# Two attention forms inside one Trainium2 kernel: the values become the stationary operand, and the division by the sum moves ahead of the product

## The reference

```python
def block_attention(q, k, v, blk, n_back, with_prev, sink=None):
    s = jnp.einsum('bnqhgd,bnkhd->bnhgqk', qb, kb) * (dh ** -0.5)   # masked by distance
    m = s.max(-1)                                  # mixers 0 and 3: also over the sink
    p = jnp.exp(s - m[..., None])
    l = p.sum(-1)                                  # mixers 0 and 3: + exp(sink - m)
    o = jnp.einsum('bnhgqk,bnkhd->bnqhd', p, vb) / l
    ...
def mixer_a(x, w_qkv, b_qkv, sinks, w_o, b_o, cos, sin):   # mixers 0 and 3
    ...
    return o.reshape(B, S, nq).astype(x.dtype) @ w_o + b_o
```

## Time and profile before

| | us |
|---|---|
| median of 3 runs (lowest, highest) | 2353.24 (2352.29, 2353.77) |
| profiled execution, its own time | 2353.32 |
| its span, first to last instruction | 2351.5 |
| TensorE busy | 2308.6 (98%) |
| VectorE busy | 1451.2 (62%) |
| ScalarE busy | 1306.0 (56%) |
| GpSimd busy | 328.9 (14%) |
| mean granted TensorE clock | 0.998 of full |

### The profile page before, as it was taken

How to read it: one execution, slowest core, us unless ns; L and a number is a source line. 1 busy time by engine, 2 the same in 40 slices (tenths; PEclk the granted TensorE clock), 3 DMA queues, 4 the chain that set the end, 5 groups by cost and what they waited for, 6 DMA issues and landing times.

```text
span 2351.5 us, 36560 instructions
## 1 busy us (share of the span) xinstructions
PE 2308.6 (98%) x15272; PEld 2066.8 (88%) x15272; DVE 1451.2 (62%) x2217; ACT 1306.0 (56%) x1958; POOL 328.9 (14%) x307
## 2 busy tenths in 40 slices
PE   7999999999999999999999999999999999999999
PEld 6799978888899888998789989899899898998998
DVE  6655555546645546555765467575687686765875
ACT  5554465555644556445564467565665675655654
POOL 0100032211100313001010002343000013530000
PEclk9999999999999999999999999999999999999999
DMA  6255543333455534555345554344455453444553
GB/s 266 90 208 187 180 178 135 140 139 126 179 184 193 197 135 161 194 183 197 120 165 194 186 181 153 138 164 165 179 183 194 175 184 122 166 163 161 201 193 126
DMA packets 58180, 398.92 MB, mean 170 GB/s; under 512 B 6816, under 2 KB 7072, under 8 KB 11680
## 3 DMA queue, kind: packets, MB, share of 16 engines
q1 hardware_dynamic: 56864, 393.75, 46.2%
q10 hardware_dynamic: 1152, 2.83, 0.3%
HBM read 395.51 MB, written 1.05 MB: 169 GB/s over the span
## 4 chain that ended last, share of the span: by engine, by line
PE 83%; DVE 8%; ACT 6%; POOL 2%; issue 1%; DMA 1%; SPq 0%; ACTq 0%; DVEq 0%; POOLq 0%
PE b L1280 12%; PE b L1282 12%; PE b L1281 12%; PE b L1178 12%; PE b L1179 12%; PE b L1180 12%; PE b L1183 5%; PE b L1187 4%; DVE wlo L1931 3%; ACT whi L1581 2%; PE b L1246 1%; ACT b L1577 1%; DVE xb L2230 1%; PE b L1247 1%; ACT S L1578 1%
## 5 line engine op out<-in xcount | busy, mean ns | idle before, releaser
L1931 DVE TENSOR_TENSOR wlo<-raw,whi 128x2048 fp32r<-128x2048 f32 x362 | 843.1, 2333 | 447.9 <-ACT whi L1581 447.6
L1581 ACT ACTIVATE whi<-raw 128x2048 fp32r<-128x2048 f32 x362 | 690.5, 1913 | 427.2 <-PE b L1282 231.0
L1280 PE MATMUL b<-xh,whi 128*128 128x256 f32 x2560 | 723.9, 283 | 0.6
L1282 PE MATMUL b<-xh,wlo 128*128 128x256 f32 x2560 | 712.5, 278 | 0.0
L1281 PE MATMUL b<-xl,whi 128*128 128x256 f32 x2560 | 711.5, 278 | 0.0
L1280 PEld LDWEIGHTS b<-xh,whi 128*128 128x128 f32 x2560 | 480.3, 188 | 5.2 <-DVE wlo L1931 2.7
L1281 PEld LDWEIGHTS b<-xl,whi 128*128 128x128 f32 x2560 | 481.4, 188 | 1.9
L1282 PEld LDWEIGHTS b<-xh,wlo 128*128 128x128 f32 x2560 | 481.1, 188 | 0.0
L1178 PE MATMUL b<-whi,xh 128*128 128x512 f32 x640 | 263.0, 411 | 1.5 <-DVE wlo L1931 1.5
L1178 PE MATMUL b<-whi,oh 128*128 128x512 f32 x656 | 259.1, 395 | 0.6 <-DVE ol L2221 0.6
L1179 PE MATMUL b<-wlo,oh 128*128 128x512 f32 x656 | 256.1, 390 | 0.0
(11 more groups left out here) (238 smaller groups left out, 2900.0 us busy)
## 6 DMA issues: line engine op xcount, KB each, us to landing
raw<-in_w SPq DMA_DIRECT2D x362, 1024.0 KB, 4.8
gt<-in_rows SPq DMA_DIRECT2D x8, 512.0 KB, 4.1
bt<-in_rows SPq DMA_DIRECT2D x8, 512.0 KB, 5.2
abq<-in_rows ACTq DMA_DIRECT2D x2, 768.0 KB, 6.2
x<-in_x SPq DMA_DIRECT2D x1, 1024.0 KB, 6.8
bc<-in_rows SPq DMA_DIRECT2D x4, 256.0 KB, 5.1
out<-x SPq DMA_DIRECT2D x4, 256.0 KB, 2.1
msk<-in_masks SPq DMA_DIRECT2D x1, 768.0 KB, 21.4
```

Of the source, the lines that this page charges most:

```text
L1280: pe.matmul(out, wh[:, k, cs], ah[:, kk, :], start=kk == 0 and s == 0, stop=False, skip_group_check=True)
L1282: last = pe.matmul(out, wl[:, k, cs], ah[:, kk, :], start=False, stop=final and k == 3, skip_group_check=True)
L1581: return ac.activation(out, i, ACT.Copy)
L1931: ve.tensor_tensor(B.wlo[r][:, :], B.raw[r][:, :], B.whi[s][:, :], ALU.subtract).then_inc(sem["loV"], 1)
```

## The change

It concerns mixers 0, 2 and 3 (`KIND` "a" and "c"); mixer 1 and the later layers keep their order (`LAG` 1).

- Order of a visit on TensorE: `probs(v-2)`, `pv(v-3)`, `score(v)`. A run of n pairs has n + 3 visits, before n + 2.
- `share`, new: after `score(v)`, VectorE takes the reciprocal for pair v-1 and divides the first head's exponentials in `S` in place, two instructions (128 and 256 columns); GpSimd does the same for the second head. The turn of a pair waits for both.
- `pv`: the stationary operand is 64 columns of values, the moving one 128 columns of turned exponentials. Head 0 goes to partitions 0 to 63 of the result, head 1 to 64 to 127; query half 0 stands in one bank, half 1 in the other. The result is already turned.
- `opair`, in place of `heads` and `opart`: VectorE copies both banks to `og`, ScalarE copies 256 columns to `oh`, GpSimd takes the rest `ol`. It stands last in its visit.
- The turned exponentials of odd pairs go to `og[2]`. The output projection waits for GpSimd's count `olo`.

```diff
+LAG = {"a": 2, "b": 1, "c": 2, "d": 1}
@@ Order.attention
-        for v in range(n + 2):
+        for v in range(n + lag + 1):
...
+            if turned and lag == 2:
+                self.step("probs", a, v - 2)
+            if v > lag:
+                self.step("pv", a, v - lag - 1, dv, n)
             if v < n:
                 ...
                 self.step("score", a, v, mask, kidx, ...)
...
             if v < n:
                 self.step("exp", a, v, sinks is not None)
...
+            if lag == 2 and 1 <= v <= n:
+                ...
+                self.step("share", a, v - 1)
+            if v > lag:
+                consume(v - lag - 1)
@@ mixer_a (mixer_bc alike, for mixer 2)
             def consume(v):
-                self.step("heads", u0, v, v // 4)
-            def tail(g):
-                self.out_part((i, g), g // 2)
-                ready[g] = True
+                self.out_pair(i, v, u0, v)
+                if v % 2:
+                    ready[v // 2] = True
@@ TensorE, rows_ready
+            if a // 2 in (0, 2, 3):
+                p.wait_ge("olo", mark["olo", (a // 2, 2 * blk + 1)])
@@ TensorE, probs
+            elif KIND[a] in "ac":
+                name = ("shared_v", "shared_g")[i]
+                p.wait_ge(name, mark[name, (a, v_)])
@@ TensorE, pv
+        if KIND[a] in "ac":
+            ...
+            for t, k, at in ((0, 0, 0), (1, 0, 128), (1, 1, 256)):
+                b = use["S", a, v_ + 3, t][0]
+                for i in range(2):
+                    c = 64 * (v_ // 2) if KIND[a] == "a" else 128 * p_ + 64 * i
+                    last = mm(B.bank[b][64 * i:64 * i + 64, 384:512], v[:, k, c:c + 64], B.turned(a, v_, i)[:, at:at + 128],
+                              k == 0, k == t)
@@ ScalarE
+    def opair(i, pair, first, v):
+        ...
+        copy(B.oh[:, pair, :], B.opair(pair)).then_inc(sem["ohi"], 1)
@@ VectorE
-    def heads(a, pair, hh):
+    def share(a, pair):
+        u, p = o.pair(a, pair)
+        s = p % 2
+        v.wait_ge("exp", mark["exp", (a, pair, 1)])
+        if pair >= 2:
+            v.wait_ge("shared_g", mark["shared_g", (a, pair - 2)])
+        ve.reciprocal(B.rl[:, s, 0:4], B.l[u % 4][:, 4 * p:4 * p + 4]).then_inc(sem["sums"], 1)
+        v.wait_ge("sums", mark["sums", (a, pair)])
+        S = B.S[2 * (pair % 2)]
+        for t, cs in enumerate((slice(0, 128), slice(129, 385))):
+            last = ve.tensor_scalar(S[:, cs], S[:, cs], B.rl[:, s, t:t + 1], None, ALU.mult)
+        last.then_inc(sem["shared_v"], 1)
+    def opair(i, pair, a, v_):
+        for t in range(2):
+            b, n = use["S", a, v_ + 3, t]
+            v.wait_ge(f"full{b}", n + 1)
+            ve.tensor_copy(B.opair(pair)[:, 128 * t:128 * t + 128],
+                           B.bank[b][:, 384:512]).then_inc(sem[f"empty{b}"], 1)
@@ GpSimd
+    def share(a, pair):
+        s, S = pair % 2, B.S[2 * (pair % 2) + 1]
+        g.wait_ge("sums", mark["sums", (a, pair)])
+        for t, cs in enumerate((slice(0, 128), slice(129, 385))):
+            last = ge.tensor_scalar(S[:, cs], S[:, cs], B.rl[:, s, 2 + t:3 + t], None, ALU.mult)
+        last.then_inc(sem["shared_g"], 1)
+    def opair(i, pair, a, v):
+        g.wait_ge("ohi", mark["ohi", (i, "pair", pair)])
+        ge.tensor_tensor(B.ol[:, pair, :], B.opair(pair), B.oh[:, pair, :], ALU.subtract).then_inc(sem["olo"], 1)
```

More of the change, by code:

```diff
@@ L550, in attention @@
                     self.counts("exp", (a, v, i))
[L551 to L556, removed]
+            if turned and lag == 1:
                 self.step("probs", a, v - 1)
@@ L573, in attention, with out_pair @@
             tail(g)
+    def out_pair(self, i, pair, a, v):
+        self.counts("ohi", (i, "pair", pair))
+        self.counts("olo", (i, pair))
+        self.step("opair", i, pair, a, v)
     def out_part(self, key, source):
@@ L682, in consume @@
                         if i == 2:
-                            self.step("heads", u, gr, hh)
+                            self.out_pair(i, 4 * hh + gr, u, gr)
+                            if gr % 2:
+                                ready[2 * hh + gr // 2] = True
                         else:
@@ L1401, in pv @@
             return
+        if KIND[a] in "ac":
+            for t in range(2):
+                b, n = use["S", a, v_ + 3, t]
+                p.wait_ge(*o.copied[a, v_, t])
+                p.wait_ge(f"empty{b}", n)
+            for t, k, at in ((0, 0, 0), (1, 0, 128), (1, 1, 256)):
[4 more added lines that the diff above has]
+                              k == 0, k == t)
+                if k == t and v_ + 3 >= pairs:
+                    last.then_inc(sem[f"full{b}"], 1)
+            return
         for i in range(2):
@@ L1405, in pv @@
             p.wait_ge(f"empty{b}", n)
[L1406 removed]
+            c = 128 * p_ + 64 * i
             pt, out = B.PT[i], B.bank[b][:, 384:512]
@@ L1707, in probs @@
     def probs(first, v):
-        b, n = use["T", first, v + 1, 0]
+        b, n = use["T", first, v + LAG[KIND[first]], 0]
         a.wait_ge(f"full{b}", n + 1)
-        copy(B.PT[0][:, 0:384], B.bank[b][:, 0:384]).then_inc(sem[o.copied[first, v, 0][0]], 1)
+        copy(B.turned(first, v, 0)[:, 0:384], B.bank[b][:, 0:384]).then_inc(sem[o.copied[first, v, 0][0]], 1)
     def rise(u, p):
@@ L1715, in rise @@
         act(e, e, ACT.Exp).then_inc(sem["stat_a"], 1)
+    def opair(i, pair, first, v):
+        for t in range(2):
+            b, n = use["S", first, v + 3, t]
+            a.wait_ge(f"empty{b}", n + 1)
+        copy(B.oh[:, pair, :], B.opair(pair)).then_inc(sem["ohi"], 1)
     def opart(key, source):
@@ L2147, in heads @@
         v.wait_ge("exp", mark["exp", (a, pair, 1)])
-        i = v.mine(ve.reciprocal(B.rl[:, s, 0:4], B.l[u % 4][:, 4 * p:4 * p + 4]))
-        values(a, pair, 1)
-        v.wait_ge("own_v", i)
-        for i in range(2):
-            c = 128 * p + 64 * i
-            src, gone = values(a, pair, i)
-            r = B.rl[:, s, 2 * i:2 * i + 2].unsqueeze(2).broadcast_to([128, 2, 64])
-            ve.tensor_tensor(B.og[hh][:, :, c:c + 64], src, r, ALU.mult).then_inc(sem[gone], 1)
+        if pair >= 2:
[7 more added lines that the diff above has]
+    def opair(i, pair, a, v_):
+        for t in range(2):
+            b, n = use["S", a, v_ + 3, t]
+            v.wait_ge(f"full{b}", n + 1)
+            ve.tensor_copy(B.opair(pair)[:, 128 * t:128 * t + 128],
+                           B.bank[b][:, 384:512]).then_inc(sem[f"empty{b}"], 1)
     def merge(u, p, g):
@@ L2476, in vector_program @@
             "center": center, "affine": affine, "meansq": meansq, "rms": rms, "sinks": sinks, "scale_x": scale_x, "kv_in": kv_in, "rope_v": rope_v, "q_bias": q_bias,
-            "score": score, "probs": probs, "heads": heads, "merge": merge, "rise": rise, "weights": weights,
+            "score": score, "probs": probs, "share": share, "opair": opair, "merge": merge, "rise": rise, "weights": weights,
             "opart": opart, "gate": gate, "hlo": hlo, "taps": taps, "gate2": gate2, "gm_squares": gm_squares,
@@ L2821, in sm, with turned, opair @@
         return self.small[:, a:a + n]
+    def turned(self, a, pair, i):
+        return self.og[2][:, i, :] if KIND[a] in "ac" and pair % 2 else self.PT[i]
+    def opair(self, pair):
+        return self.og[pair // 4][:, pair % 4 // 2, 256 * (pair % 2):256 * (pair % 2) + 256]
     def act(self, x):
```

45 lines of the change are left out of this document (22 added, 23 removed).

## The result

The changed kernel takes **2374.04 us** (median of 4 runs, 2373.04 to 2377.39) against 2352.76 for the kernel before (4 runs beside it): a ratio of 1.0094, 95% interval 1.0083 to 1.0106. It is 0.9% slower. The forecast was 2354 with a range of 2341 to 2366; the time lies outside it, 20 us above the number. The profiled execution took 2374.39 us, its span is 2372.6.

A forecast was written before the change was run, and what follows sets the result against it. TensorE, busy 98% of the span, was taken to bound the kernel. -9.7 - 5.2 - 4.8 + 8.2 + 3.0 + 8.0 + 1.5 = +1.0 on 2353.3 gave 2354 us; 8-in-10 range 2341 to 2366.

The forecast's parts named there:

- Relief: TensorE's visits in mixers 0, 2 and 3 shorten from 2.87 to 2.47 us (-9.7); twelve `opart` go (-5.2).
- that rival: In `pv` the column halves run one after another, 0.67 us more each, 16 in all: 2370 us; chance 0.09.
- old waits: TensorE's existing waits in mixers 0, 2 and 3, where `opart` or a turn waited for VectorE or ScalarE, go: -4.8 us.
- first turns: In mixers 0 and 3 the turns of visits 2 and 3 come late, 1.5 us each: +3.0 together.
- turns of visits 6, 7, 8: In mixers 0 and 3, behind six products, the second head's turn waits 1.2 us for GpSimd's division in each visit.
- (b): In mixers 0 and 3 the output projection's first row waits 4.0 us for the last result `ol`: +8.0 together.
- I take s + 3.0 for GpSimd: GpSimd's two divisions end 3.0 us after s, when TensorE finishes a visit's scores; ends s + 2.6 and s + 5.2.
- GpSimd is locked out: Rival: VectorE's `wlo` comes between GpSimd's two divisions and holds the second by 2.2 us: 2363 us; chance 0.14.
- a sign that the prediction is wrong: Turns waiting where 12 products lie between visits; with 12 or 18 products nothing was to be lost.
- (c): In mixer 2 one `wlo` right after `share` and one before GpSimd's last difference cost +1.5 us together, ends 0 and 4.
- (a): Turns wait for divisions behind six products: three visits each in mixers 0 and 3, one in mixer 2 (1.0): +8.2 us.
- The waits don't come or are short: Rival: GpSimd finishes at s + 2.6, shrinking the waits (about 2347), or relief counts alone (2334); put at 2343 us, chance 0.29.

The follow-up runs named there:

- Kernel 7: Only mixer 2 changed, with divisions and older sums (`opair`) issued ahead of the scores, against the kernel before: 2347.28 us, ratio 0.9978.
- Experiment 3: The changed kernel with all four divisions of a pair of visits on VectorE at the same place, none on GpSimd: 2361.63 us.
- experiment 1: The changed kernel with the divisions issued ahead of fill and score, right behind the products with the values: 2358.32 us.
- Experiments 4 and 5: The kernel before, TensorE held before the first output projection row in mixers 0 and 3 by four or two GpSimd products: 2364.86 and 2358.38 us.
- experiment 2: The changed kernel with the divisions and the older sums (`opair`) both issued ahead of the scores: 2355.93 us.
- (9): Changed kernel, divisions and older sums ahead of scores; in mixers 0 and 3 visit 4's older work no longer waits for the queries' second half: 2373.37 us.
- kernel 6: The change made in mixer 2 only, mixers 0 and 3 as in the kernel before: 2353.37 us, ratio 1.0004.

## Why the prediction was wrong

Mechanism and places of most waits were right; the sum missed 20 us because waits on divisions were priced too low, mostly through GpSimd, and because nothing stood in it for the clock. By place, measured less predicted, it missed 6.8 us in mixer 0 (9.0 against 2.2), 8.6 in mixer 3 (10.8 against 2.2), 3.6 in mixer 2 (0.1 against -3.5) and 1.3 in mixer 1, where it had no term.

**Relief: right.** The products with the values take 0.806 us, start to next start; I took 0.86. The two heads' column halves run side by side (their records start 0.01 us apart in pairs), so that rival is out. The turn takes 0.75 instead of 0.63, I had 0.65. By TensorE's blocks, mixer 0 saves 8 x (2.87 - 2.42) + 4 x 0.44 = 5.4 us; my sum has 5.0 a mixer. Kernel 7 shows it in time: mixer 2 is 5.4 us shorter there.

Mixer 0, term by term, from the distances between TensorE's starts in the changed kernel:

| | predicted | measured |
|---|---|---|
| products, transposes of `og` | -5.0 | -5.4 |
| old waits | -1.9 | -1.8 |
| first turns (visit 2: 0.8 + 2.7) | +1.5 | +3.5 |
| turn of visit 4, small ones | 0 | +1.1 |
| first row | +4.0 | +4.2 |
| turns of visits 6, 7, 8 (1.65, 1.63, 1.47) | +3.6 | +4.8 |
| half clock, twice | 0 | +3.0 |
| sum | +2.2 | +9.4 (+9.0 by the cut) |

**The first row's wait (b): right in place, and nearly in size.** 4.2 us in mixer 0 against 4.0, and the same idle time, 4.09, in mixer 3. The chain is the one forecast, VectorE's copy behind scores and divisions, ScalarE's copy behind the exponentials, then GpSimd's difference at 75.05. But GpSimd's own two divisions ended only then (73.44 + 1.64), just behind ScalarE's copy, while the forecast had them done a quarter of a microsecond ahead of it. Here are VectorE, then ScalarE, then GpSimd, of the changed kernel before the row at 75.88:

```profile
73.37 0.66 DVE L2188 TENSOR_SCALAR S<-S,rl 128x128 f32<-128x128 f32 x2
73.96 0.47 DVE L2195 COPY og<-b 128x128 f32<-128x128 f32 x2
```
```profile
74.53 0.42 ACT L1609 ACTIVATE oh<-og 128x256 fp32r<-128x256 f32 x1
```
```profile
73.44 1.64 POOL L2582 TENSOR_SCALAR S<-S,rl 128x128 f32<-128x128 f32 x2 [6.08 <-DVE rl L2184]
75.05 0.72 POOL L2587 TENSOR_TENSOR ol<-og,oh 128x256 fp32r<-128x256 f32 x1
```

**The step that failed first: "I take s + 3.0 for GpSimd".** I priced its two divisions at 1.1 to 1.3 us from a product of 256 columns and a 512-column division of 1.49. They take 1.65, so the undisturbed pair is done at s + 3.4 (64.89 + 1.65, with s at 63.17), and 3.6 where a `wlo` comes between. That is what my rival "GpSimd is locked out" said: I gave it 0.14. A `wlo` came between in four visits: in one of mixer 0 at 51.40, in one of mixer 3 (where the second head's turn came 2.7 us late as well, at 1152.95), and in mixer 2 at 849.41 and 895.53. Each pair took about 1.95 us over the undisturbed one; three of them, 5.8 us together, stood in TensorE's way, and behind the one at 849.41 TensorE stood idle for only 0.42. I had counted the late first turns as "1.5 us each" without putting that rival's price there. Experiment 3 takes GpSimd out and gains 12.4 us, experiment 1 gives the divisions a head start and gains 15.7. The list of places was short too. In mixer 2's second run visit 2 stands behind six products as visit 4 does, and turns waited behind 12 products at 899.18 and behind 18 at 853.06, which I had named as a sign that the prediction is wrong. The Trainium skill, GPSIMD Engine Reference (Specifications), says that GpSimd shares its SBUF interfaces with VectorE instructions that have two SBUF inputs. `wlo` is one, and the pair of 3.60 us around it agrees: the price here is the length of the `wlo` less the overlap.

**The step that was missing: the clock.** My waits cost their length and no more. Experiments 4 and 5 show that this is wrong by 1.6 us for a wait of 4 us, and by 1.3 to 1.5 for one of 2 us in one of two places. In the changed kernel it makes 1.5 + 1.5 us in mixer 0 (nine products over 3.7 us that take 2.2 at full clock, and the scores and products from 55.55). Mixer 3 had 13.7 us at the lower level where mixer 0 had 6.8, about 1.3 us more of it in work that TensorE had to do (products and scores ahead of the row, from 1168.03 to 1171.09, took 3.06 us in place of 1.74 in mixer 0); this is the larger part of what it lost beyond mixer 0 (10.8 against 9.0). The Trainium skill, TensorE: Matmul & The Clock Gate (Why this matters for your kernels), warns of idle gaps between bursts of products because they bring the lower clock. The trace agrees behind mixer 0's wait of 4.1 us and behind both waits of experiment 4 (in mixer 3 of the changed kernel the drop began ahead of the wait), and the page would have been grounds for a term for the two row waits that I forecast at 4.0. That waits of 2.4 us drew the drop too is in this trace.

**Mixer 2 (c):** predicted -3.5 (its share of the relief, old waits, +1.0 of (a), +1.5), measured +0.1 from the 124th to the 135th conversion. Its waits on divisions are 5.6 us by the trace, not 2.5: the first heads wait 0.6 in two visits, the second heads 0.7, 0.8, 2.0 and 0.8. That explains 3.1 of the 3.6 us. The other 0.6 is relief and old waits that I put at 6.0 and kernel 7 shows as 5.4. The remaining 1.3 us of the part up to the 135th conversion are the wait on GpSimd's rotation in mixer 1.

**One rival's number.** "The waits don't come or are short" gives 2350 by its own terms (2354.3 less seven times 0.4 and twice 0.7), not 2347. The forecast doesn't use it.

**What stays open.** Whether the sink mixers can gain at all. With the best order (2) they still lose 1.8 and 2.4 us in the profiled execution, which was 2.3 us faster than the median: row wait, visit 7 with its fill under a `wlo`, one half clock each. The row's wait could not be moved forward (9). Writing the sinks elsewhere than on GpSimd wasn't tried.

## What to carry to other kernels

When work moves ahead of the product that needs it, price the new wait at the *slowest* case of the engine it moves to, and look for what of its neighbour may come between two of its instructions; two small divisions took 0.66 us on VectorE and 1.65 to 3.6 on GpSimd. Put new producers first in their engine's visit, not behind work of a younger visit: the same instructions in that order were worth 15.7 us here. A wait of TensorE of some microseconds isn't always paid with its length alone; count a half-clock stretch behind it, 1.3 to 1.6 us each here, and take such a change stage by stage, since one stage (mixer 2, 0.22% faster) may win what the others lose.

## What the runs showed of the hardware

- Products of 64 stationary columns for two heads, on separate columns of the array: 12 f32 records in 0.806 us with 128 moving columns, against 1.38 us with the exponentials as stationary operand.
- GpSimd's fill of 4 columns took 0.19 us alone and 2.31 beside a `wlo` that had started 0.02 us earlier (experiment 2), more than the 1.25 of the earlier trace rows.
- VectorE's 256-column division took 0.46 us in the changed kernel, with GpSimd's division running beside it, and 0.35 in experiment 3, where GpSimd had none.
- The clock's drop is not fixed by one wait's length: 2.1 us of waiting was followed by it in one of two like places of the same run, and 1.77 us on a turn in mixer 2 in kernel 6 but not in the changed kernel. In experiment 3 it stood at 0.50 for 13.7 us at one place.
